# Softmax sums inverted as a 32x33 tile that DMAs gather and spread, in 22 of 24 head pairs

## The reference

```python
xn = rms_norm(h, norm1_g)
proj = xn @ w_in
fq, fk, fv, ff, cq, ckv, krope, sq, sk, sv, gates = jnp.split(proj, offsets, axis=-1)
out_a = causal_block_attention(fq, fk, fv, log_decay)      # "Fox": causal, with a decay
out_b = causal_block_attention(q, k, v_mla)                # "MLA": q, k, v from a latent
out_c = sliding_window_attention(sq, sk, sv, swa_sinks, alibi_slopes(SWA_Q_HEADS))
g = jax.nn.sigmoid(gates.reshape(B, L, N_BRANCH, D_MODEL))
y = jnp.einsum('blnc,ncd->blnd', branches, w_branch)
h = h + jnp.sum(g * y, axis=2) @ w_o
# then: h = h + (silu(conv(u)_gate) * conv(u)_val) @ w_down, with u = rms_norm(h) @ w_up
```

## Time and profile before

| | |
|---|---|
| median of 3 runs | 1982.04 us (1978.26 to 1982.62) |
| the profiled execution, span from first to last instruction | 1979.4 us |
| its own time around the span | not given; the median lies 2.6 us above the span |
| PE busy | 1914.7 us, 97% |
| DVE busy | 1159.0 us, 59% |
| ACT, POOL busy | 766.2 us, 39%; 1025.5 us, 52% |
| mixers | about 25 to 555 us and 1008 to 1550 us |
| feed-forward parts | about 555 to 1008 us and 1550 to 1979 us |
| TensorE clock granted, mean | 0.995 |

### The profile page before, as it was taken

The page is one execution under the profiler, slowest core; times in us unless marked ns, Lnnn a source line. Parts: engine busy times, 40 slices in busy tenths (PEclk is TensorE's granted clock), DMA queues, the critical chain, the costliest instruction groups (busy, mean ns, idle before and its releaser), DMA issues.

```text
span 1979.4 us, 36478 instructions
## 1 busy us (share of the span) xinstructions
PE 1914.7 (97%) x14396; PEld 1817.1 (92%) x14396; DVE 1159.0 (59%) x2121; ACT 766.2 (39%) x1514; POOL 1025.5 (52%) x1306
## 2 busy tenths in 40 slices
PE   7899999999999999999998999999999999999999
PEld 7889998888999999999997899988889999999887
DVE  7665476787465666552256654767874655665411
ACT  5455666655223222220044556666553232222100
POOL 7655454544364444544477455544443645445553
PEclk9999999999999999999999999999999999999999
DMA  4212121211232322332332121112112423323332
GB/s 149 75 44 65 54 65 44 63 45 55 65 129 85 97 86 86 97 93 93 93 109 76 43 65 54 63 46 65 45 53 65 141 86 97 97 86 96 96 97 96
DMA packets 44802, 156.30 MB, mean 79 GB/s; under 512 B 5012, under 2 KB 5268, under 8 KB 44504
## 3 DMA queue, kind: packets, MB, share of 16 engines
q1 hardware_dynamic: 44488, 153.75, 24.7%
q10 hardware_dynamic: 144, 0.22, 0.0%
HBM read 149.63 MB, written 4.26 MB: 78 GB/s over the span
## 4 chain that ended last, share of the span: by engine, by line
PE 77%; DVE 12%; ACT 4%; issue 3%; POOL 2%; DMA 1%; SPq 0%; DVEq 0%; ACTq 0%; POOLq 0%
PE ps L1357 20%; PE ps L1360 19%; PE ps L1362 19%; PE ps L1588 5%; PE ps L1372 2%; PE ps L1368 2%; PE ps L1371 2%; PE ps L1376 2%; DVE osum L1993 1%; DVE rstd L1691 1%; PE ps L1540 1%; PE ps L1501 1%; POOL wl L817 1%; DVE ps L1962 1%; DVE square L1686 1%
## 5 line engine op out<-in xcount | busy, mean ns | idle before, releaser
L817 POOL TENSOR_TENSOR wl<-raw,wh 128x256 fp32r<-128x256 f32 x1076 | 798.7, 773 | 746.5 <-DVE wh L1670 739.9
L1357 PE MATMUL ps<-xh,wh 128*128 128x264 f32 (+1 forms) x2880 | 810.7, 303 | 12.5 <-DVE wl L1750 9.4
L1360 PE MATMUL ps<-xl,wh 128*128 128x264 f32 (+1 forms) x2880 | 764.3, 286 | 0.0
L1362 PE MATMUL ps<-xh,wl 128*128 128x264 f32 (+1 forms) x2880 | 585.4, 285 | 0.0
L1357 PEld LDWEIGHTS ps<-xh,wh 128*128 128x128 f32 x2880 | 546.7, 190 | 31.1 <-issue 18.3
L1360 PEld LDWEIGHTS ps<-xl,wh 128*128 128x128 f32 x2880 | 547.4, 190 | 17.0 <-issue 8.9
L1362 PEld LDWEIGHTS ps<-xh,wl 128*128 128x128 f32 x2880 | 451.2, 190 | 0.0
L1670 DVE CAST wh<-raw 128x1024 fp32r<-128x1024 f32 x270 | 206.6, 765 | 176.0 <-PE ps L1357 89.1
L1588 PE MATMUL ps<-pt,vx 128*128 128x512 f32 (+7 forms) x480 | 157.8, 409 | 3.9 <-ACT pt L1274 2.3
L1985 DVE TENSOR_TENSOR ps<-ps,cst 128x128 f32<-128x128 f32 (+6 forms) x240 | 74.8, 313 | 145.3 <-PE ps L1546 111.0
L1274 ACT ACTIVATE pt<-ps 128x256 f32<-128x256 f32 (+5 forms) x224 | 78.5, 363 | 112.5 <-DVE ps L1985 111.2
(11 more groups left out here) (194 smaller groups left out, 3440.9 us busy)
## 6 DMA issues: line engine op xcount, KB each, us to landing
raw<-weights SPq DMA_DIRECT2D x270, 512.0 KB, 3.5
h<-tokens SPq DMA_DIRECT2D x4, 528.0 KB, 6.9
h<-tokens SPq DMA_DIRECT2D x8, 264.0 KB, 6.0
residual<-h SPq DMA_DIRECT2D x8, 264.0 KB, 5.0
h<-residual SPq DMA_DIRECT2D x8, 264.0 KB, 5.9
out<-h SPq DMA_DIRECT2D x8, 256.0 KB, 4.7
cst<-constants SPq DMA_DIRECT2D x1, 1048.0 KB
extra<-positions SPq DMA_DIRECT2D x18, 4.1 KB
```

The lines of the kernel that those rows point to most:

```text
L817: ins = nc.gpsimd.tensor_tensor(wl[c % SPLIT][:, part], raw[:, c % RAW, part], wh[c % SPLIT][:, part].bitcast(F32), ALU.subtract)
L1357: a = nc.tensor.matmul(out, a_hi, x_hi[:, sl], start=first, stop=False)
L1360: nc.tensor.matmul(out, a_hi, x_lo[:, sl], start=False, stop=False)
L1362: ins = nc.tensor.matmul(out, a_lo, x_hi[:, sl], start=False, stop=last)
```

## The change

In all pairs but pair 11 (so in 11 of a layer, 22 in all) the sums are inverted once each instead of 64 times. SP gathers one row of `osum` for each head by DMA (step "fold", at b+15) into 32 partitions of 33 numbers, in a part of `krr` that was free. DVE inverts that 32x33 tile in one instruction ("recip", at b+18). SP stores it to DRAM ("unfold", at b+18), waits for that, and reads each head's row back 64 times into its 64 rows of `osum` ("spread", two DMAs, at b+22). DVE's "heads" moves from b+21 to b+30, with ACT's and POOL's "head copy" 9 indices later too. Pair 6 keeps its place at 279 and pair 11 is as before.

The diff also rewrites the chunk code so that other engines could take part in the cast and the low part. The constants leave that work as it was: DVE casts, POOL subtracts, at the same places (`MIX_HIGH, FFN_HIGH = "dve", "dve"`; `MIX_DVE, FFN_DVE = 0, 0`; `NUDGE = {}`). Its code is left out here.

```diff
+FOLD = [3, 7, 13]
+FOLD_N = 2 * T // (P - MQ)
+UNFOLDED = [11]
+def folded(j):
+    return j not in UNFOLDED
...
         i = b + ST_HEAD + 4 + PV_LAG + 2
-        for q in range(4):
-            put(i + q, 6, "recip", j, q)
+        if folded(j):
+            put(i, 2, "fold", j)
+            put(i + FOLD[0], 6, "recip", j, 0)
+            put(i + FOLD[0], 7, "unfold", j)
+            put(i + FOLD[1], 8, "spread", j)
+            i += FOLD[2] - 4
+        else:
+            for q in range(4):
+                put(i + q, 6, "recip", j, q)
         if j >= OT_RING:
             i = max(i, end_of["y", (JOBS[j - OT_RING][0], KD - 1)] - 3)
         put(i + 4, 2, "heads", j)
         put(i + 4, 8, "head copy", j)
...
+    inverse = nc.dram_tensor("inverse", (DEPTH, len(JOBS), 2, T), F32, kind="Internal").ap()
+    def fold(j):
+        return krr[fold_at:P, j % 2 * FOLD_N:(j % 2 + 1) * FOLD_N]
...
+                    elif s[0] == "fold":
+                        sp.wait_ge(heads_copied.sem, heads_copied.at(l, j, 1))
+                        sp.wait_ge(meta_heads_copied.sem, meta_heads_copied.at(l, j))
+                        for e in range(2):
+                            sp.dma_start(fold(j)[a:a + half_rows, :],
+                                         osum[e * HD:e * HD + 1, :].rearrange("o (r c) -> o r c", c=FOLD_N)).then_inc(
+                                sums_folded.sem, sums_folded.tick((l, j), 16))
+                    elif s[0] == "unfold":
+                        sp.wait_ge(dve_step.sem, dve_step.at(l, "recip", j, 0))
+                        sp.dma_start(inverse[l, j, :, :].rearrange("e (r c) -> (e r) c", c=FOLD_N), fold(j)).then_inc(
+                            inverse_stored.sem, inverse_stored.tick((l, j), 16))
+                    elif s[0] == "spread":
+                        sp.wait_ge(inverse_stored.sem, inverse_stored.at(l, j))
+                        for e in range(2):
+                            sp.dma_start(osum[e * HD:(e + 1) * HD, :],
+                                         inverse[l, j, e:e + 1, :].broadcast_to([HD, T])).then_inc(
+                                inverse_spread.sem, inverse_spread.tick((l, j), 16))
...
                     elif s[0] == "recip":
+                        if folded(j):
+                            dve.wait_ge(sums_folded.sem, sums_folded.at(l, j))
+                            nc.vector.reciprocal(fold(j), fold(j)).then_inc(
+                                dve_step.sem, dve_step.tick((l, "recip", j, 0)))
+                            continue
...
                     elif s[0] == "heads":
-                        dve.wait_ge(dve_step.sem, dve_step.at(l, "recip", j, 3))
+                        if folded(j):
+                            dve.wait_ge(inverse_spread.sem, inverse_spread.at(l, j))
+                        else:
+                            dve.wait_ge(dve_step.sem, dve_step.at(l, "recip", j, 3))
```

More of the change, by code:

```diff
@@ L185, in __init__, with step_name @@
         self.raw = None
+def step_name(step):
+    words = [step[0]]
+    for x in step[1:]:
+        if isinstance(x, Tile):
+            words.append(f"{x.kind}{x.m[0]}{x.m[1]}" if isinstance(x.m, tuple) else f"{x.kind}{x.m}")
+        elif not isinstance(x, dict):
+            words.append(str(x))
+    return " ".join(words)
 def mixer_plan():
@@ L383, in weight_plan, with in_mixer, high_by, low_by @@
     return b
-PLAN = weight_plan(mixer_plan()["order"])
+MIXER = mixer_plan()["order"]
+PLAN = weight_plan(MIXER)
 CHUNKS = DEPTH * len(PLAN) // BLK
 assert len(PLAN) % BLK == 0
+HIGH_AT = {"dve": 0, "act": 0, "pool": 0}
+LOW_AT = {"dve": 0, "pool": 0}
+POOL_PIECE = 256
+FIRST = 3
+MIX_HIGH, FFN_HIGH = "dve", "dve"
+MIX_DVE, FFN_DVE = 0, 0
+def in_mixer(c):
+    i = c * BLK % len(PLAN)
+    return i < len(MIXER)
+def high_by(c):
+    return "dve" if c < FIRST else MIX_HIGH if in_mixer(c) else FFN_HIGH
+def low_by(c):
+    d = CW if c == 0 else 0 if c < FIRST else MIX_DVE if in_mixer(c) else FFN_DVE
+    return {"dve": (0, d), "pool": (d, CW)}
 def build(nc, W, H, PRM, CST, POS, OUT, SCR, counts):
@@ L620, in frees, with chunk_raw, high_done, low_done @@
         return gate_used, t.m
+    def chunk_raw(c):
+        return s_raw[c % RAW], 16 * (c // RAW + 1)
+    def high_done(c):
+        s = chunk_high[high_by(c)]
+        return s.sem, s.at(c)
+    def low_done(c):
+        return [(chunk_low[e].sem, chunk_low[e].at(c)) for e, (a, b) in low_by(c).items() if b > a]
     previous = {}
@@ L1039, in _, with high_part, advance @@
             logarithms()
+            def high_part(c):
+                if c >= CHUNKS or high_by(c) != "act":
+                    return
+                act.wait_ge(*chunk_raw(c))
+                if c >= SPLIT:
+                    act.wait_ge(s_start, c - SPLIT + 2)
+                copy(wh[c % SPLIT][:, :], raw[:, c % RAW, :]).then_inc(
+                    chunk_high["act"].sem, chunk_high["act"].tick((c,)))
+            def advance(l, i):
+                n = l * LB + i
+                if n % BLK == HIGH_AT["act"] and n >= BLK:
+                    high_part(n // BLK + AHEAD)
             def high_input(l, k):
@@ L1304, in square_residual, with advance_by @@
                         residual_squared.sem, residual_squared.tick((l, which, k)))
+                count = {"n": n_blocks}
+                def advance_by(n):
+                    for _ in range(n):
+                        advance(l, count["n"])
+                        count["n"] += 1
                 for k in range(KD):
+                    advance_by(2 * KD if k == 0 else KD if k > 1 else 0)
                     act.wait_ge(residual_updated.sem, residual_updated.at(l, "wo", k))
@@ L1334, in _ @@
                     act.wait_ge(tile_ready.sem, tile_ready.at(l, "up", 2 * FT - 1))
-                    for k in range(KD):
+                for k in range(KD):
+                    advance_by(FT)
+                    if l + 1 < DEPTH:
                         act.wait_ge(residual_updated.sem, residual_updated.at(l, "dn", k))
@@ L1347, in weights @@
                 if n % BLK == 0:
-                    pe.wait_ge(s_lo, c + 1)
+                    for sem, value in low_done(c):
+                        pe.wait_ge(sem, value)
                 a = n % BLK * P
```

87 lines of the change are left out of this document (65 added, 22 removed).

## The result

The changed kernel took 1995.63 us (median of 4 runs, 1995.13 to 1997.06) beside 1981.61 us before on the same chip, a ratio of 1.0077 with a 95% interval of 1.0063 to 1.0091. The forecast was 1973 us, with 1954 to 1989 as the range: wrong in sign, and outside the range by 7 us.

The account below looks back on a forecast made before the run. PE, busy 97%, was taken as the bound, waiting for what stands behind DVE's reciprocals. Per layer 6.05 gained plus 0.85 clock minus 1.0 and 1.5 gave 4.4 us, about 9 in both: 1973 us, 8-in-10 range 1954 to 1989.

Parts of the forecast that it names:

- SP's own time, some 3 us a pair, is free: SP's issuing of the new DMAs was claimed to cost nothing, since SP waits for POOL at nearly every load.
- Gathered 4.1 us after the copies: Pair 8's gathering DMAs: 0.58 us issue each, 3.5 us landing, so the tile is ready near 414.4 us.
- Rival 4: Small DMAs land as late as 5.9 us, DVE stands at new reciprocals and heads: 1995 us; chance 0.08.
- Pair 8, 1.5 us foreseen: Fewer reciprocals ahead of L1830 and L1832 move the reduction up, shortening PE's wait: gain 1.5 us a layer.
- Pair 6, 0.95: Without the first reciprocal ahead of L1832, PE's wait for `rawt` nearly goes: gain 0.95 us a layer.
- Pair 0 with the clock, 0.7 + 0.85: Heads leaves its place ahead of the shift, gaining 0.7 us; less clock loss after PE's wait adds 0.85.
- Pair 1, 0.8: L1691 on DVE gets shorter as POOL's head copy moves away: gain between nothing and 1.0 us, taken as 0.8.
- Pairs 2, 5 and 9, 2.1 together: Waits of 0.5 to 2 us behind their reciprocals shrink: 0.7 us gained in each pair, 2.1 a layer.
- Pair 4, 1.0: A weight load between gathering and store delays the spread, so heads and head copy are late: cost 1.0 us.
- Pair 1, 1.5: POOL's head copy stands behind `yq` and a chunk, so ACT's PVM and an exponential are late: cost 1.5 us.
- pair 5's head copy: With POOL's later order, ACT was claimed at most 1 us late in pairs 0, 3, 5 and 9.
- Rival 3: ACT stands at PVM for POOL's late head copy, PE losing 2 us in five pairs: 1988 us; chance 0.12.

Follow-up runs that it names:

- e1: Changed kernel with no pair folded, all reciprocals and heads back in place, the rest of the new code kept: 1982.52 us.
- e5: Changed kernel with the fold DMAs of pairs 2, 6, 7 and 9 one index earlier in SP's order, ahead of the weight load: 1974.18 us.
- e9: Changed kernel with only pairs 0, 2, 6, 8, 9 folded, SP issuing the fold ahead of the weight load as in e5: 1970.16 us.
- e12: Changed kernel with only pairs 2, 6, 7 and 9 folded, SP's order left as changed (fold behind the weight load): 1994.11 us.
- e3: Kernel without the division in pairs 0 to 10: no reciprocal, no DMA, heads at the old place: 1970.11 us.
- e10: Nothing folded, no DMA, all reciprocals in place; only heads and head copy of pairs 0 and 2 stand later than before: 1976.17 us.
- e2: Nothing folded, no DMA, reciprocals in place; heads and head copy of pairs 0 to 10 late as in the changed kernel: 1981.99 us.
- e7: Changed kernel with new reciprocal and unfold 7 instead of 3 indices behind the fold, spread 9 instead of 7, heads unmoved: 2032.66 us.

## Why the prediction was wrong

The steps of three kernels, in us per mixer (first layer, second layer), pair 5 against e1:

```
                        changed      e5           e9
pair 0  (80-112)       -2.3 -2.1   -2.2 -2.1   -2.2 -2.1
pair 2  (136-160)       1.0  1.1   -0.6 -0.6   -0.6 -0.6
pair 4  (208-240)       0.5  0.5    0.5  0.5    0    0
pair 5  (240-264)       1.4  2.2    1.6  1.4    0    0
pair 6  (264-296)       0.4  1.5   -1.2 -1.1   -1.2 -1.3
pair 7  (296-336)       2.3  2.2    0.5  0.3    0    0
pair 8  (336-360)      -0.2 -0.5   -0.2 -0.5   -0.5 -0.5
pair 9  (360-408)       3.0  3.8   -1.3 -1.3   -1.3 -1.3
```

- **The step that failed** is the sentence "SP's own time, some 3 us a pair, is free: it sits waiting for POOL at nearly every load." It does sit there, and for that reason nothing behind the load can be issued. I looked at what stands between fold and unfold (pair 4), not at what stands ahead of the fold. In four pairs the load does, and the fold left 4 us late. Changed against e5 this is 9.3 us in the first layer and 11.3 in the second by the steps, 21.4 us by the medians. e12, with these pairs alone, lost nearly what the changed kernel did (ratio 1.0067 and 1.0077).
- **"Gathered 4.1 us after the copies"** was too late for most pairs and too early for the four. Both DMAs had landed 2.4 to 2.6 us after the copies in pairs 0, 3, 4 and 8, 2.4 and 3.9 in pair 10, 3.5 to 4.6 in pairs 1 and 5, and 7.3 to 8.4 in pairs 2, 6, 7 and 9. The landing is 2.8 us from issue in the median, below the 3.5 I took; the issue was as taken. Rival 4 had the sign and even the time, 1995, and in four pairs about its 7.1 us to the gathered tile, but by a mechanism that is not there: it wanted landings of 5.9 us in every pair. That it hit the time is luck. The Trainium skill (DMA: Bandwidth & Descriptors, Anatomy of one DMA, which describes DMAs issued from GpSimd) says that a semaphore wait happens on the issuing sequencer before dispatch. The trace agrees for SP: of the delay in the four pairs 4 us lie between copies and issue. Only about 1 us, the later landing behind a load, lies in the DMA.

The three DMA and reciprocal rows of the changed kernel (ns min/median/max; landing in us):

```profile
L845 SPq DMA_DIRECT2D krr<-osum x44: 544/589/1393, 100.1 to 1493.4; - x44
...
DMA to landing us min/median/max: 1.7/2.8/3.3
...
L2149 DVE RECIPROCAL krr<-krr x22: 358/360/365, 104.4 to 1495.3; 32x33 f32<-32x33 f32 x22
```

- **Gains.** Pair 8, 1.5 us foreseen: 1.0 to 1.4 by e3, of which late heads give 0.9 back (e5: 0.2 and 0.5). Pair 6, 0.95: 1.2. Pair 0 with the clock, 0.7 + 0.85: 2.2. PE's idle time there fell by 0.7 us, as taken; the clock at 100 to 120 us came back whole, 1.00 for 0.91, and I had taken half of its 1.8 us (0.85 in the sum, where half is 0.9). Pair 1, 0.8: nothing. DVE's L1852 (L1691 before) did shrink from 1.73 to 0.71 us once POOL's head copy was away, but PE had no wait behind it. Pairs 2, 5 and 9, 2.1 together: 0.6 at pair 2, 1.3 at pair 9, a loss of 1.4 at pair 5. Pair 2's 0.6 comes from late heads alone (e10).
- **Costs.** Pair 4, 1.0: 0.5. Pair 1, 1.5: nothing; ACT waits 3.3 us at pair 2's PVM, as foreseen, and no step shows it. The longest of its waits, 4.0 us, is at pair 6's PVM for pair 5's head copy, which I had put at 1 us at most; it is beside the 1.4 us of pair 5 in the table. Pair 7 pays too (0.3 and 0.5 in e5, 1.0 and 1.1 in e2). Rival 3 had a grain of truth: late heads cost 3.7 us in pairs 4, 5, 7 and 8 of the first layer and win 2.4 in pairs 0 and 2 (e2).
- **The sum without the queue** came out near: 1973 foreseen, 1974.2 measured in e5. That is in part luck, since pair 0's clock was taken too low and the costs of pairs 5 and 7 were not in it, while pair 1's cost was.

## What to carry to other kernels

A queue that is idle because it waits is not free: whatever is put behind a waiting DMA issue inherits the wait, so for each new DMA read what stands ahead of it on its engine and when that is released, and put it ahead if the old one cannot go earlier anyway. Moving a consumer away from a wait (e7) is no cure while the rest of the chain passes the same queue, because the wait turns up at the next instruction with something worse behind it. And fold only where a wait of PE stands behind the removed work: by the steps five of eleven pairs, with the order put right, gave more than all, and two of the five (pairs 0 and 2) owe most or all of it to late heads. When a wait of PE is priced, look at the granted clock behind it too: here it was, by estimate, a third of the four pairs' loss and over half of the step at e7's pair 7.

## What was not expected of the hardware

A 32x33 reciprocal takes 0.36 us where 128x132 takes 0.958: 0.6 us for 99 columns. If time goes with columns alone, that leaves about 0.16 us that do not depend on length, an estimate from these two sizes. A DMA of 2.1 KB from one partition landed 1.7 us after issue when SP had issued no weight load in the 2 us before it, and 3.0 to 3.3 us when one stood 0.43 us ahead (the first DMA of each pair, changed kernel; once 2.1 in the first case). The row's median of 2.8 us mixes the two. Steps of PE can be longer than the wait that made them (8.5 us for a wait of PE of 4.1 in e7), with a granted clock below full speed behind the wait. e7's first mixer, by stretch as in the earlier trace rows:

```profile
60.00:580.00 520.00, 485.31 (x3495) 447.83 (x3494) 287.12 (x674) 274.34 (x591) 249.79 (x295) 0.98 0.20 61
```

In e5 the granted clock was 1.00 in both mixers.
